# Two FFN tiles computed as a pair, and half of the low parts made on GpSimd

## The reference, cut to what matters

```python
def rmsnorm(x, g, eps=RMS_EPS):
    y = xf * lax.rsqrt(jnp.mean(xf * xf, axis=-1, keepdims=True) + eps)
    return (y * g).astype(x.dtype)

def swiglu(h, w1, w3, w2):
    return (jax.nn.silu(h @ w1) * (h @ w3)) @ w2

y = y + swiglu(rmsnorm(y, norm_ffn_g[l]), ffn_w1[l], ffn_w3[l], ffn_w2[l])   # w1, w3: 1024 x 2816
```

## Time and profile before

| | us |
|---|---|
| median of 3 runs (lowest, highest) | 2050.66 (2047.96, 2051.35) |
| the profiled execution | 2048.34 |
| its span, first to last instruction | 2046.6 |
| mean granted TensorE clock | 0.965 |
| TensorE busy | 1942.4, 95% |
| VectorE busy | 742.4, 36% |
| ScalarE busy | 450.3, 22% |
| GpSimd busy | 141.5, 7% |

### The profile page before, as it was taken

The page is one execution under the profiler, slowest core; times in us unless marked ns, Lnnn a source line. Parts: engine busy times, 40 slices in busy tenths (PEclk is TensorE's granted clock), DMA queues, the critical chain, the costliest instruction groups (busy, mean ns, idle before and its releaser), DMA issues.

```text
span 2046.6 us, 26656 instructions
## 1 busy us (share of the span) xinstructions
PE 1942.4 (95%) x11462; PEld 1622.3 (79%) x11462; DVE 742.4 (36%) x1203; ACT 450.3 (22%) x714; POOL 141.5 (7%) x149
## 2 busy tenths in 40 slices
PE   7999989899889999999998999799988999999998
PEld 5755556655659999999996999565565999999998
DVE  2099843312444332233334131631245333223222
ACT  3200231101422211111222114430133211121111
POOL 3001000000000000000004332200000000000000
PEclk9999986699999999999999999899999999999999
DMA  6322130150021112312120343411402211221120
GB/s 226 124 70 66 43 124 2 45 205 30 13 103 59 65 57 77 103 61 69 57 93 18 103 64 81 157 67 52 185 11 103 82 55 57 97 89 61 63 90 32
DMA packets 32036, 161.71 MB, mean 79 GB/s; under 512 B 8584, under 2 KB 9224, under 8 KB 18016
## 3 DMA queue, kind: packets, MB, share of 16 engines
q1 hardware_dynamic: 24032, 122.16, 18.1%
q0 software_dynamic: 7936, 38.60, 5.1%
HBM read 150.07 MB, written 10.42 MB: 78 GB/s over the span
## 4 chain that ended last, share of the span: by engine, by line
PE 92%; DVE 4%; ACT 2%; issue 1%; DMA 0%; POOL 0%; ACTq 0%; DVEq 0%
PE G L614 84%; PE Q L614 4%; PE S L614 3%; ACT rstd L1099 1%; DVE front L1417 1%; PE Q L1032 1%; DVE work L1721 1%; DVE h_split L1725 1%; ACT work L1099 0%; PE Q L884 0%; DVE stats L1836 0%; DMA front<-in_mem 0%; DVE front L1849 0%; DVE front L1619 0%; DVE stats L1659 0%
## 5 line engine op out<-in xcount | busy, mean ns | idle before, releaser
L614 PE MATMUL G<-h_split,w_split 128*128 128x320 f32 x5184 | 768.6, 310 | 10.6 <-DVE h_split L1725 10.5
L614 PEld LDWEIGHTS G<-h_split,w_split 128*128 128x128 f32 x5184 | 764.4, 189 | 12.8 <-issue 8.9
L614 PE MATMUL G<-front,ring 128*128 128x512 f32 (+2 forms) x1792 | 486.9, 434 | 12.4 <-DVE front L1417 7.0
L614 PEld LDWEIGHTS G<-front,ring 128*128 128x128 f32 x1792 | 279.5, 193 | 218.9 <-issue 212.6
L614 PE MATMUL G<-g_split,w_split 128*128 128x320 f32 x2112 | 310.4, 309 | 0.0
L614 PEld LDWEIGHTS G<-g_split,w_split 128*128 128x128 f32 x2112 | 309.9, 188 | 0.0
L1453 DVE TENSOR_TENSOR w_split<-ring,w_split 128x1024 fp32r<-128x1024 f32 (+2 forms) x152 | 164.4, 1083 | 359.3 <-ACT w_split L1099 359.3
L1099 ACT ACTIVATE w_split<-ring 128x1024 fp32r<-128x1024 f32 (+2 forms) x172 | 164.4, 957 | 517.8 <-PE G L614 517.8
L1503 DVE SCALAR_TENSOR_TENSOR front<-front,par 128x512 f32<-128x512 f32 x240 | 111.6, 546 | 0.1
L1099 ACT ACTIVATE work<-G 128x640 f32<-128x640 f32 x52 | 36.7, 706 | 331.9 <-PE G L614 331.9
L1737 DVE TENSOR_TENSOR work<-work,G 128x640 f32<-128x640 f32 x44 | 36.1, 821 | 183.9 <-PE G L614 183.9
(11 more groups left out here) (211 smaller groups left out, 1118.1 us busy)
## 6 DMA issues: line engine op xcount, KB each, us to landing
ring<-in_w_up0a SPq DMA_DIRECT2D x11, 1024.0 KB, 4.8
ring<-in_w_up0b SPq DMA_DIRECT2D x11, 1024.0 KB, 4.8
ring<-in_w_up1a SPq DMA_DIRECT2D x11, 1024.0 KB, 4.7
ring<-in_w_up1b SPq DMA_DIRECT2D x11, 1024.0 KB, 4.8
front<-in_mem_k POOLq DMA_DIRECT2D x8, 1024.0 KB, 11.7
front<-in_mem_v POOLq DMA_DIRECT2D x8, 1024.0 KB, 14.4
ring<-in_w_down0a SPq DMA_DIRECT2D x8, 704.0 KB, 4.1
ring<-in_w_down0b SPq DMA_DIRECT2D x8, 704.0 KB, 4.1
```

Source lines behind the costliest of these rows:

```text
L614: return nc.tensor.matmul(out, lhsT, rhs, start=start, stop=stop, **kw)
```

## The change

In the first half of each layer's FFN the first two tiles are made together: for each row block TensorE does the six matmuls of the even tile and then the six of the odd tile. The low parts of row blocks 1, 3, 5 and 7 are made by GpSimd, those of 0, 2, 4 and 6 by VectorE. `applied` is raised only by VectorE's four, a new semaphore `h_odd` by GpSimd's four. On GpSimd the four instructions stand behind the issue of the cross-attention caches' loads, ahead of the clearing of `forget` in layer 0 and ahead of the output stores in layer 1.

```diff
-               + [(f"q0.{j}", 1) for j in range(4)] + [("ffn0", 8), ("mix1", 8)]
+               + [(f"q0.{j}", 1) for j in range(4)] + [("ffn0", 4), ("mix1", 8)]
...
-               + [(f"q1.{j}", 1) for j in range(4)] + [("ffn1", 8)]):
+               + [(f"q1.{j}", 1) for j in range(4)] + [("ffn1", 4)]):
...
             cross_caches(0, TILE0["evout"])
+            def odd_low_parts(l):
+
+                for k in range(1, KD, 2):
+                    pool.wait_ge(h_hi, KD * l + k + 1)
+                    nc.gpsimd.tensor_tensor(hs[:, 1, k, :], raw_tile(k), hs[:, 0, k, :].bitcast(F32), ALU.subtract)\
+                        .then_inc(h_odd, 1)
+
+            odd_low_parts(0)
             nc.gpsimd.memset(forget[:, :].bitcast(F32), 0.0).then_inc(run_zero, 1)
...
             cross_caches(1, TILE0["odout"] + 7)
+            odd_low_parts(1)
...
+            def split_pair(n, p, rhs, normed, odd):
+
+
+                for j in range(2):
+                    begin(n + j)
+                pe.wait_ge(split, p + 2)
+                for k in range(KD):
+                    if k % 2:
+                        pe.wait_ge(h_odd, odd + k // 2 + 1)
+                    else:
+                        pe.wait_ge(applied, normed + k // 2)
+                    for j in range(2):
+                        for wpart, xpart in ((0, 0), (0, 1), (1, 0)):
+                            w = ws[:, j, wpart, k * P:(k + 1) * P]
+                            for f in range(2):
+                                fr = slice(f * HT, (f + 1) * HT)
+                                m = mm(GF[(n + j) % 2][:, fr], w, rhs[:, xpart, k, fr],
+                                       k == 0 and wpart + xpart == 0, k == KD - 1 and wpart == 1)
+                        if k == KD - 1:
+                            m.then_inc(tile_done, 1)
...
-                    first = APPLIED[f"ffn{l}"] - KD + 1 if half == "a" else None
-                    for j in range(2):
-                        split_product(t0 + j, j, p0 + j, KD, hs, normed=first if j == 0 else None)
+                    if half == "a":
+                        split_pair(t0, p0, hs, APPLIED[f"ffn{l}"] - KD // 2 + 1, l * KD // 2)
+                    else:
+                        for j in range(2):
+                            split_product(t0 + j, j, p0 + j, KD, hs)
...
                 for k in range(KD + 1):
                     if k < KD:
-                        if k >= 4:
-                            dve.wait_ge(applied, APPLIED[f"ffn{l}"] - KD + k - 3)
+                        if k >= 4 and k % 2 == 0:
+                            dve.wait_ge(applied, APPLIED[f"ffn{l}"] - KD // 2 + k // 2 - 1)
+                        elif k >= 4:
+                            dve.wait_ge(h_odd, l * KD // 2 + k // 2 - 1)
                         v.scalar_tensor_tensor(out=raw_tile(k), in0=x[:, k, :], scalar=pr(f"ffn{l}", k),
                                                in1=rstd[:, m % 2, :], op0=ALU.mult, op1=ALU.mult).then_inc(h_raw, 1)
-                    if k:
+                    if k % 2:
                         dve.wait_ge(h_hi, KD * l + k)
```

More of the change, by code:

```diff
@@ L331, in build @@
         h1_hi, h1_split = sem("h1_hi"), sem("h1_split")
-        h_raw, h_hi = sem("h_raw"), sem("h_hi")
+        h_raw, h_hi, h_odd = sem("h_raw"), sem("h_hi"), sem("h_odd")
         ones_in, const_in, par_in, mem_in, pads_in = map(
```

## The result

The changed kernel took 2054.12 us (median of 20 runs, 2050.61 to 2055.38), the kernel before 2049.36 (20 runs, 2044.8 to 2051.35). The ratio is 1.0021, 95% interval 1.0014 to 1.0027: 2.9 to 5.5 us slower, so the difference is clear of zero, and it lies across the 0.2% (4.1 us) up to which I had forecast no change. The forecast was 2052.5 us, the range 2048.0 to 2056.0. The profiled execution took 2053.21 us for a span of 2051.4.

A forecast was written before the change was run, and what follows sets the result against it. TensorE, busy 95% of the span, was taken as the bound, except at the FFN entry. Pair and weights' wait +1.2 and one clock fall +1.7 gave +2.9 us; from mean 2049.6, forecast 2052.5 us, range 2048.0 to 2056.0.

The forecast's parts named there:

- Part 1: FFN entry: pairing two tiles keeps TensorE busy and, taken alone, wins 3.55 us over both layers.
- Part 2: Ahead of tile 2: TensorE waits 2.17 us per layer for its weights; with the pair's gain, sum +1.2 us.
- Part 3: Four low parts on GpSimd: turns with VectorE slow the producer, the pair's slack covers it; worth 0.
- rival 1: First matmuls of tile 2: clock falls in both layers, layer 1's pair has a long low stretch; +5.4 us, chance 0.2.
- Part 4: Clock in the new wait ahead of tile 2: 0 to 1.7 us per layer; one fall taken, +1.7 us.
- Rival 2: Ahead of tile 2: weights are ready within the pair's last 0.88 us, no wait; -4 us, chance 0.05.
- rival 3: Inside the pair: GpSimd's low parts come late and TensorE waits; +7 us in the heavy case, chance 0.05.
- rival 4: Start of layer 0's pair: low stretch 1.7 us instead of 5.08, layer 0 better by 1.7; no chance stated.

The follow-up runs named there:

- e5: The changed kernel plus two matmuls with unread results in the wait ahead of tile 2; ratio to the kernel before 1.0007 (0.9997 to 1.0018).
- e8: The kernel before plus four matmuls with unread results ahead of the FFN; ratio to the kernel before 0.9994 (0.9986 to 1.0003).
- e7: The changed kernel with blocks 4 to 7 tile by tile, all low parts on VectorE, four unread matmuls ahead of the FFN; ratio to before 0.9972.
- e3: The changed kernel with blocks 0 to 3 in pairs, then blocks 4 to 7 tile by tile; ratio to before 0.9991 (0.9982 to 1.0000).
- e1: The changed kernel with all eight low parts on VectorE, so the pair alone; ratio to before 1.0021 (1.0012 to 1.0030).
- e2: The changed kernel without the pair: GpSimd's four low parts, tiles one after the other; ratio to before 1.0040 (1.0027 to 1.0054).
- e9: The changed kernel plus four matmuls with unread results ahead of the FFN; ratio to before 0.9990 (0.9982 to 0.9999).
- e4: The changed kernel plus four matmuls with unread results in the wait ahead of tile 2; ratio to before 1.0014 (1.0005 to 1.0023).
- e10: Repeat of GpSimd's four low parts without the pair, tiles one after the other; ratio to before 1.0040 (1.0027 to 1.0053).
- e11: GpSimd's four low parts without the pair, plus one unread matmul behind each of blocks 3 to 6 of tile 0; ratio to before 1.0037.

## Why the prediction was right, and where it was off

The direction and the range held, and the mechanism of parts 1 to 3 did. The bound did not quite: I gave 0.76 to a change within 4.1 us, and the measured 2.9 to 5.5 us lie across it. What happened is rival 1, to which I gave 0.2: the clock fell in both layers, and layer 1's pair started with a low stretch almost as long as layer 0's. Its +5.4 is nearer to the measured 4.76 than my +2.9. The measured time lies in the range because the range had been drawn to take in rival 1, not because the central sum was right; and the range isn't quite the sum of its own terms, which give 2047.4 to 2055.3. By its steps:

- **Part 1, the pair.** Forecast: no idle between the 96 matmuls, tile 0 done 15.96 and 15.16 us after the first. Measured: one record of 96, 15.78 and 15.66. Layer 1's difference is the slow stretch, 4.85 us instead of 3.48: 0.7 us that the rows of before could not fix (e5's layer 1 had 6.19). e8 and e7 show the reading behind it: a full clock is worth 0 to the kernel before and 2.0 us per layer to one that keeps TensorE busy.
- **Part 2, the weights.** Forecast 2.17 us of wait, measured 2.12 in both layers, at the named place. e3 takes it away, and the fall behind it with it, and turns +4.55 into -2.03. This is the step that decided.
- **Part 3, GpSimd.** Forecast: the turns make the producer slower, the pair's slack hides it, worth 0. e1: 0.01 us. e2: without the pair to hide it, +4.9. The change's low parts on VectorE start 3.64 us apart (3.66 forecast per two blocks). Its forecast of 12.5 us for the last low part holds: 622.89 + 1.56 - 612.00 = 12.45.
- **Part 4, the clock.** This term was mis-sized. I bounded it by 0 to 1.7 us per layer and took one fall in two layers; it fell in both, and in both of e1. The price of one fall was right (1.7 forecast, 1.5 by e5 and e9). With two falls and layer 1's longer stretch, the steps give 1.2 + 3.4 + 0.7 = +5.3, against 4.55 by the trace; tile 2 took 8.88 and 8.82 us from its first matmul to its end instead of 7.26, so the two falls cost 3.2 and not 3.4, and the end of tile 0 and the weights behind it each came 0.1 to 0.2 us per layer sooner than the steps have them. The Trainium skill's sentence on idle gaps (TensorE: Matmul & The Clock Gate, section HAM oscillation) gave +1.2; five of the six waits of this length in the traces of the change, e1 and e9 contradict it.
- **Rival 2** (no wait), **rival 3** (GpSimd late) and **rival 4** (a shorter low stretch in layer 0: it was 5.10 us, 5.08 forecast) did not happen in the change. Rival 3's mechanism shows where TensorE comes to the blocks sooner: in e3 its matmuls wait 0.26 and 0.42 us for GpSimd, and in e9 its weight load waits 0.39.

## What to carry to other kernels

When two tiles are interleaved, they also end together, and whatever was refilled behind the first tile's end loses its cover: look at what waits for the first one before pairing. Interleave only as long as the producer is behind, then finish tile by tile; that order kept the gain and dropped the wait. An idle time of TensorE can cost more than itself: here one of 2.12 us cost 1.5 more in low clock behind it, most times but not each time. So price both, and remember that a low clock shows in the time only where TensorE is the bound (e8 against e7).

## What the runs showed that I had not expected

- The same idle time of 2.12 us between dense matmuls let the clock fall in five cases (both layers of the change and of e1, layer 1 of e9) and not in a sixth (layer 0 of e9). Each low stretch behind it lasted 3.4 us and cost 1.5 to 1.6. What decides whether the clock falls stays open.
- A float32 matmul of 128 x 512 (not fp32r as in the split products) stands as two records, and four in a row take 3.60 us, 0.90 each: twice what I had assumed in e4.
- A change at the FFN entry can move the time of a stage 700 us later by 2.7 us with no instruction of it changed (e2, e10, e11), through the clock alone as far as the windows tell; in e9 that way is 2.6 us shorter instead. Differences of 0.1% between kernels can hold such a part, so the yardstick and the measured ratio have to be read together.
